# Two chunked recurrences: decay sums, exponentials and weighted operands of a chunk placed in the last steps of the chunk before

## What is computed

```python
def step(state, inp):
    r_t, w_t, k_t, v_t, a_t, b_t = inp
    sa = jnp.einsum('bhvk,bhk->bhv', state, a_t)
    state = (state * w_t[:, :, None, :] + sa[..., None] * b_t[:, :, None, :]
             + v_t[..., None] * k_t[:, :, None, :])
    return state, jnp.einsum('bhvk,bhk->bhv', state, r_t)
...
w = -jax.nn.softplus(-(w0_d + jnp.tanh(dlo) @ w2_d)) - 0.5
decay = jnp.exp(-jnp.exp(w.astype(jnp.float32)))
o = wkv7_scan(rh, heads(decay), kh, vh, -kk, b_vec, reverse)
o = (head_group_norm(o, ln_g, ln_b) + bonus).reshape(B, S, RWKV_WIDTH)
```

## Time and profile before

| | |
|---|---|
| runs of the kernel | 3740.72, 3750.13, 3750.52 us; median 3750.13 us |
| the profiled execution | 3743.04 us, its span 3741.3 us |
| mean granted clock of TensorE | 0.964 |
| PE busy | 3462.3 us, 93% of the span |
| DVE busy | 1727.7 us, 46% |
| ACT busy | 1111.7 us, 30% |
| POOL busy | 329.3 us, 9% |

### The profile page before, as it was taken

How to read it: one execution, slowest core, us unless ns; L and a number is a source line. 1 busy time by engine, 2 the same in 40 slices (tenths; PEclk the granted TensorE clock), 3 DMA queues, 4 the chain that set the end, 5 groups by cost and what they waited for, 6 DMA issues and landing times.

```text
span 3741.3 us, 61040 instructions
## 1 busy us (share of the span) xinstructions
PE 3462.3 (93%) x27176; PEld 2747.7 (73%) x27176; DVE 1727.7 (46%) x2528; ACT 1111.7 (30%) x1789; POOL 329.3 (9%) x342
## 2 busy tenths in 40 slices
PE   8999999889988888898999999989899999999998
PEld 7678677667766775366887788768677778878876
DVE  4443455555555555645334533552454522253235
ACT  4323324333343331022113311333332311132124
POOL 1222231111111111100000000000000000000000
PEclk9999999999998998999999999999999999999999
DMA  3241242211111203321112211222102211121122
GB/s 137 73 131 57 91 168 67 67 46 45 37 56 44 78 25 124 105 94 55 46 51 73 86 50 51 96 92 86 45 30 90 73 45 45 57 90 62 51 68 96
DMA packets 89975, 269.83 MB, mean 72 GB/s; under 512 B 11552, under 2 KB 12080, under 8 KB 89712
## 3 DMA queue, kind: packets, MB, share of 16 engines
q1 hardware_dynamic: 78960, 230.26, 18.6%
q0 software_dynamic: 10752, 35.66, 2.8%
HBM read 219.73 MB, written 46.14 MB: 71 GB/s over the span
## 4 chain that ended last, share of the span: by engine, by line
PE 77%; DVE 10%; issue 7%; ACT 3%; POOL 1%; DMA 1%; SPq 0%; DVEq 0%; POOLq 0%; ACTq 0%
PE ps L355 72%; DVE X L364 3%; PE ps L358 3%; PE ps L354 2%; DVE AR L364 2%; DVE SM L375 1%; POOL AR L364 1%; DVE OTB L364 1%; ACT HH L361 1%; DVE HL L364 1%; ACT W L1966 0%; ACT WS L361 0%; DMA qk_d<-AR 0%; ACT HT L1144 0%; DVE SA L364 0%
## 5 line engine op out<-in xcount | busy, mean ns | idle before, releaser
L355 PE MATMUL ps<-HH,WS 128*128 128x512 f32 (+1 forms) x3232 | 1001.4, 391 | 0.0
L355 PEld LDWEIGHTS ps<-HH,WS 128*128 128x128 f32 (+1 forms) x3232 | 607.8, 188 | 129.9
L355 PE MATMUL ps<-HL,WS 128*128 128x512 f32 x1616 | 639.3, 396 | 10.1 <-DVE HL L364 10.1
L364 DVE TENSOR_TENSOR WS<-W,WS 128x1024 fp32r<-128x1024 f32 (+1 forms) x245 | 300.3, 1226 | 639.5 <-ACT WS L361 639.1
L355 PE MATMUL ps<-WS,SA 128*128 128x512 f32 x2112 | 493.4, 394 | 42.5 <-DVE SA L364 42.5
L361 ACT ACTIVATE WS<-W 128x1024 fp32r<-128x1024 f32 (+1 forms) x245 | 257.6, 1051 | 904.6 <-PE ps L355 892.2
L355 PEld LDWEIGHTS ps<-WS,SA 128*128 128x128 f32 x2112 | 399.3, 190 | 133.8 <-DVE SA L364 31.6
L355 PEld LDWEIGHTS ps<-HL,WS 128*128 128x128 f32 x1616 | 303.8, 188 | 75.1 <-issue 10.5
L355 PE MATMUL ps<-WS,HL 128*128 128x512 f32 x576 | 211.8, 402 | 13.2 <-DVE WS L364 8.7
L355 PE MATMUL ps<-WS,HH 128*128 128x512 f32 x640 | 206.9, 400 | 13.5 <-DVE HL L364 4.8
L355 PE MATMUL ps<-HL,HI 128*128 128x512 f32 (+1 forms) x512 | 209.5, 409 | 3.9 <-POOL WL L364 2.8
(11 more groups left out here) (280 smaller groups left out, 4516.4 us busy)
## 6 DMA issues: line engine op xcount, KB each, us to landing
W<-in_w_fd SPq DMA_DIRECT2D x88, 512.0 KB, 3.3
AR<-rw_d SPq DMA_DIRECT2D x104, 256.0 KB, 4.0
W<-in_w_fg SPq DMA_DIRECT2D x44, 512.0 KB, 3.3
W<-in_w_fu SPq DMA_DIRECT2D x44, 512.0 KB, 3.3
W<-in_w_tok SPq DMA_DIRECT2D x24, 512.0 KB, 3.3
rw_d<-X POOLq DMA_DIRECT2D x40, 256.0 KB, 3.3
X<-in_x SPq DMA_DIRECT2D x16, 512.0 KB, 9.2
W<-in_w_g SPq DMA_DIRECT2D x16, 512.0 KB, 3.7
```

The source lines that it names most:

```text
L355: return pe.e.matmul(o, l, r, start=start, stop=stop)
L364: return e.e.tensor_tensor(o, x, y, op)
```

## The change

A chunk's preparation moves out of its own first step into the last steps (`u` = 1) of the preceding chunk.

- TensorE: the decay sums of chunk i + 1 (`sums`) come behind B, three steps ahead of the chunk's start. The first step of a chunk now has the transposes T0 and T1, the second T2 and T3.
- DVE: the subtraction (`less_own`) is in B's step, the products `At` and `Rt` (`weighed`) in the step of O and U. Removing the mean (`centred`) and summing the squares (`spread`) of chunk i - 1 are behind the copies of T0 and T2 of chunk i.
- ACT: the three exponentials (`exps`) are in B's step, `e2` first; `e1` is written into `c.KT`, which is free by then, since `c.E[1]` is `c.Kt` and still read.
- POOL: `Bt` and `Kt` wait for the state matmuls S of the preceding chunk, which read the same buffers, and no longer for each other; the squares go to `c.D4` and stand behind them.
- SP: the next loads are issued one step later.

The numbers of steps stay, but for one more at the very beginning. Chunk 0 has no preceding chunk: its preparation stands alone in that step.

```diff
                 yield
+                yield
                 if i < 7:
                     sp.wait_ge(*at(f"ve_s{d}", "T", i, 2))
                     sp.wait_ge(*at(f"ae_s{d}", "T", i, 3))
                     sp.wait_ge(*at(f"ge_s{d}", "K", i))
                     load(i + 1)
-                yield
...
-            for i in range(8):
-                v_ = c.vb[i % 2]
+            def sums(i):
                 b = take(pe, PEs, "tc", i)
                 pe.wait_ge(*at(f"dma_ld{d}", i))
                 mm(pe, ps[:, b, :], c.TC, c.sg, True, True).then_inc(*pe.sig(PEs, "tc", i))
-                yield
+
+            sums(0)
+            yield
+            for i in range(8):
+                v_ = c.vb[i % 2]
                 for n, x_ in enumerate((c.At, c.Rt, c.Bt, c.Kt)):
+                    if n == 2:
+                        yield
                     b = take(pe, PEs, "T", i, n)
                     if n < 2:
...
                     for h in range(4):
                         x = mm(pe, ps[src, b, 64 * h:64 * h + 64], c.V2[dst, h, :], c.TT[dst, h, dst], True, True)
                     x.then_inc(*pe.sig(PEs, "B", i, u))
+                    if u and i < 7:
+                        sums(i + 1)
                     yield
                     bo = take(pe, PEs, "O", i, u, n=2)
                     state(pe, c, bo, u, 1)
...
+            def less_own(i):
                 ve.wait_ge(*at(PEs, "tc", i))
                 if i:
-                    ve.wait_ge(*at(VEs, "vr", i - 1))
+                    ve.wait_ge(*at(VEs, "A", i - 1))
                 tt(ve, c.E[2], ps[:, bank(PEs, "tc", i), :], c.sg, ALU.subtract).then_inc(*ve.sig(VEs, "tc", i))
-                yield
+
+            def weighed(i):
                 ve.wait_ge(*at(AEs, "e2", i))
                 ve.wait_ge(*at(f"dma_ld{d}", i))
                 tt(ve, c.At, c.kkn, c.E[2], ALU.mult).then_inc(*ve.sig(VEs, "A", i))
+                ve.wait_ge(*at(AEs, "e0", i))
                 tt(ve, c.Rt, c.r, c.E[0], ALU.mult).then_inc(*ve.sig(VEs, "R", i))
+
...
+            less_own(0)
+            weighed(0)
+            yield
+            for i in range(8):
                 ve.wait_ge(*at(PEs, "T", i, 0))
                 ve.e.tensor_copy(c.ART[:, :, 0, :], hv(bank(PEs, "T", i, 0))).then_inc(
                     *ve.sig(VEs, "T", i, 0, frees=(PEs, "T", i, 0)))
+                if i:
+                    centred(i - 1)
+                yield
                 ve.wait_ge(*at(PEs, "T", i, 2))
                 ve.e.tensor_copy(c.BT, hv(bank(PEs, "T", i, 2))).then_inc(*ve.sig(VEs, "T", i, 2, frees=(PEs, "T", i, 2)))
+                if i:
+                    spread(i - 1)
                 yield
...
                     ve.wait_ge(*at(PEs, "B", i, u))
                     ve.e.tensor_copy(c.TT[src, :, dst], v3(ps[src, bank(PEs, "B", i, u), 0:256], 4)).then_inc(*done("B", i, u))
-                    yield
+                    if u and i < 7:
+                        less_own(i + 1)
+                    yield
+                    if u and i < 7:
+                        weighed(i + 1)
                     yield
...
-                mu, vr = [z[:, d * 64 + t * 8:d * 64 + t * 8 + 8] for z in (MU, VR)]
-                o3 = v3(c.OB, 8)
-                ve.wait_ge(*at(AEs, "O", i, 1))
-                red(ve, mu, o3).then_inc(*ve.sig(VEs, "mu0", i))
-                ve.wait_ge(*at(VEs, "mu0", i))
-                ts(ve, mu, mu, 1.0 / 64, None, ALU.mult, None).then_inc(*ve.sig(VEs, "mu", i))
-                ve.wait_ge(*at(VEs, "mu", i))
-                tt(ve, o3, o3, bl(mu, 64), ALU.subtract).then_inc(*ve.sig(VEs, "om", i))
-                ve.wait_ge(*at(GEs, "o2", i))
-                red(ve, vr, v3(c.E[2], 8)).then_inc(*ve.sig(VEs, "vr", i))
+            centred(7)
+            spread(7)
...
-            for i in range(8):
+            def exps(i):
                 b = bank(PEs, "tc", i)
                 ae.wait_ge(*at(VEs, "tc", i))
+                ae.e.activation(c.E[2], c.E[2], ACT.Exp, scale=-EH).then_inc(*ae.sig(AEs, "e2", i))
                 ae.e.activation(c.E[0], ps[:, b, :], ACT.Exp, scale=-EH).then_inc(*ae.sig(AEs, "e0", i))
-                ae.e.activation(c.E[1], ps[:, b, :], ACT.Exp, scale=EH).then_inc(*ae.sig(AEs, "e1", i, frees=(PEs, "tc", i)))
-                ae.e.activation(c.E[2], c.E[2], ACT.Exp, scale=-EH).then_inc(*ae.sig(AEs, "e2", i))
-                yield
+                if i:
+                    ae.wait_ge(*at(PEs, "M", i - 1, 1, 3))
+                ae.e.activation(c.KT.rearrange("p a b -> p (a b)"), ps[:, b, :], ACT.Exp, scale=EH).then_inc(
+                    *ae.sig(AEs, "e1", i, frees=(PEs, "tc", i)))
+
+            exps(0)
+            yield
+            for i in range(8):
                 ae.wait_ge(*at(PEs, "T", i, 1))
                 cp(ae, c.ART[:, :, 1, :], hv(bank(PEs, "T", i, 1))).then_inc(*ae.sig(AEs, "T", i, 1, frees=(PEs, "T", i, 1)))
+                yield
                 ae.wait_ge(*at(PEs, "T", i, 3))
                 cp(ae, c.KT, hv(bank(PEs, "T", i, 3))).then_inc(*ae.sig(AEs, "T", i, 3, frees=(PEs, "T", i, 3)))
                 yield
...
+                    if i:
+                        ae.wait_ge(*at(VEs, "vr", i - 1))
                     copy(c.D4, two(bank(PEs, "D4", i, u)), "D4", i, u)
...
                     yield
+                    if u and i < 7:
+                        exps(i + 1)
                     yield
                     copy(c.U, hv(bank(PEs, "U", i, u), 256), "U", i, u)
...
+            def squares(i):
+                ge.wait_ge(*at(VEs, "om", i))
+                tt(ge, c.D4.rearrange("p a h (g n) -> p (a h g) n", n=64), v3(c.OB, 8), v3(c.OB, 8),
+                   ALU.mult).then_inc(*ge.sig(GEs, "o2", i))
+
+            yield
             for i in range(8):
-                yield
+                e1 = c.KT.rearrange("p a b -> p (a b)")
                 ge.wait_ge(*at(AEs, "e1", i))
                 ge.wait_ge(*at(f"dma_ld{d}", i))
-                tt(ge, c.Bt, c.bb, c.E[1], ALU.mult).then_inc(*ge.sig(GEs, "B", i))
-                ge.wait_ge(*at(GEs, "B", i))
-                tt(ge, c.Kt, c.k2, c.E[1], ALU.mult).then_inc(*ge.sig(GEs, "K", i))
+                if i:
+                    ge.wait_ge(*at(PEs, "S", i - 1, 1))
+                tt(ge, c.Bt, c.bb, e1, ALU.mult).then_inc(*ge.sig(GEs, "B", i))
+                tt(ge, c.Kt, c.k2, e1, ALU.mult).then_inc(*ge.sig(GEs, "K", i))
+                yield
+                if i:
+                    squares(i - 1)
                 yield
...
-                ge.wait_ge(*at(VEs, "om", i))
-                tt(ge, v3(c.E[2], 8), v3(c.OB, 8), v3(c.OB, 8), ALU.mult).then_inc(*ge.sig(GEs, "o2", i))
+            squares(7)
```

More of the change, by code:

```diff
@@ L1457, in masked @@
                        bc(c.mask2, 2), ALU.mult).then_inc(*ve.sig(VEs, "M", i, u, h, frees=(PEs, "M", i, u, h)))
-            ve.e.memset(c.TT[dst, :, src], 0.0).then_inc(*ve.sig(VEs, "TT0"))
-            for i in range(8):
-                t = tile_of(d, i)
+            def less_own(i):
                 ve.wait_ge(*at(PEs, "tc", i))
                 if i:
-                    ve.wait_ge(*at(VEs, "vr", i - 1))
+                    ve.wait_ge(*at(VEs, "A", i - 1))
                 tt(ve, c.E[2], ps[:, bank(PEs, "tc", i), :], c.sg, ALU.subtract).then_inc(*ve.sig(VEs, "tc", i))
-                yield
+            def weighed(i):
                 ve.wait_ge(*at(AEs, "e2", i))
@@ L1469, in scan_ve, with centred, spread @@
                 tt(ve, c.At, c.kkn, c.E[2], ALU.mult).then_inc(*ve.sig(VEs, "A", i))
+                ve.wait_ge(*at(AEs, "e0", i))
                 tt(ve, c.Rt, c.r, c.E[0], ALU.mult).then_inc(*ve.sig(VEs, "R", i))
+            ve.e.memset(c.TT[dst, :, src], 0.0).then_inc(*ve.sig(VEs, "TT0"))
+            def centred(i):
+                t = tile_of(d, i)
+                mu = MU[:, d * 64 + t * 8:d * 64 + t * 8 + 8]
+                o3 = v3(c.OB, 8)
+                ve.wait_ge(*at(AEs, "O", i, 1))
+                red(ve, mu, o3).then_inc(*ve.sig(VEs, "mu0", i))
+                ve.wait_ge(*at(VEs, "mu0", i))
+                ts(ve, mu, mu, 1.0 / 64, None, ALU.mult, None).then_inc(*ve.sig(VEs, "mu", i))
+                ve.wait_ge(*at(VEs, "mu", i))
+                tt(ve, o3, o3, bl(mu, 64), ALU.subtract).then_inc(*ve.sig(VEs, "om", i))
+            def spread(i):
+                t = tile_of(d, i)
+                ve.wait_ge(*at(GEs, "o2", i))
+                red(ve, VR[:, d * 64 + t * 8:d * 64 + t * 8 + 8], c.D4.rearrange("p a h (g n) -> p (a h g) n", n=64)).then_inc(
+                    *ve.sig(VEs, "vr", i))
+            less_own(0)
+            weighed(0)
+            yield
+            for i in range(8):
                 ve.wait_ge(*at(PEs, "T", i, 0))
```

## The result

The changed kernel takes 3656.13 us (median of 4 runs, 3653.02 to 3656.53), the kernel before beside it 3750.32; the ratio is 0.9752, with a 95% interval of 0.9735 to 0.9770. Forecast were 3672, with a range from 3642 to 3706. The gain is 94 us by the medians and 86.6 us between the two profiled executions (spans of 3741.3 and 3654.7 us). A later set of five executions of the changed kernel has one of 6888 us, which no comparison here uses; the median of its other four is 3658.3 us.

The account below looks back on a forecast made before the run. TensorE, busy 93% of the span, was taken as the bound, standing still at chunk starts for late operands. 63.3 + 2 + 20 - 12 = 73 us off 3743 gives 3670, off the median 3677; forecast 3672, range 3642 to 3706.

Parts of the forecast that it names:

- waits for At and Rt, with the first chunks: TensorE's waits at chunk-start transposes for VectorE's products: 63.3 us go at 14 starts, 2 us more at the first chunks.
- clock: TensorE at chunk starts: without stillness its clock shouldn't fall, so transposes and matmuls behind shorten; 20 us, ends 0 and 28.
- new waits: Moved instructions on DVE, ACT and POOL stand ahead of the other stream's work: 0.85 us per start, 12 us lost.
- Waits that go: At 14 later chunk starts operands are ready when the transposes' turn comes: 63.3 us, 4.5 us each.
- the walk: Step-by-step timing of the chunk start without attention: transposes get about 1.5 us to spare, new waits together 0.9 us.
- The first chunks: First chunk of each direction: two exponentials leave the path to At; 2 us gained of 8.1, ends 0 and 3.
- for them I add 0.1 us each start: Small matmuls behind the chunk-start transposes also leave the slow stretch: 0.1 us per start, 1.5 us in all.
- Rival (a): DVE's queue at the chunk start stands bare 3.0 us at 14 starts, losing 42 us, not 12: 3700; chance 0.17.
- (b): TensorE's short idles suffice to keep its clock low, transposes stay at 0.22 us each: 3690; chance 0.12.
- factor of 1.6: Speedup of chunk-start transposes taken from the rows: 18.5 us won, where a factor of two would give 25 us.
- (c): Slower: every moved instruction on ACT, DVE and POOL lies bare, 8.9 us a start: 3783; chance 0.04.
- (d): More gain: new waits nil and the clock's gain at its end, 63.3 + 3 + 28 = 94 us: 3649; chance 0.09.

Follow-up runs that it names:

- filled kernel: The kernel before with 24 useless identity transposes on TensorE at each of the 14 later chunk starts, ahead of its wait for At: 3728.2 us, ratio 0.9953.

## Why the prediction was right, and where its sizes were off

The forecast was a sum; the two traces give each term of it.

| term | forecast | measured |
|---|---|---|
| waits for At and Rt, with the first chunks | 63.3 + 2 | 71.4 - 4.2 = 67.2 |
| clock | 20 | 805.8 - 775.2 = 30.6 |
| new waits | -12 | 35.4 - 46.0 = -10.6 |
| sum | 73 | 87.2 |

- **Waits that go.** Right at all 14 starts, and the walk fits: it gave the transposes 1.5 us to spare at the thinnest place, and the trace has the products end at 1281.31 and the transposes begin at 1282.78. The first chunks gained more than the 2 us priced, and more than the stated end of 3: 8.1 us became 4.2.
- **The clock** was mis-sized, beyond its stated end of 28, and it is the one term that matters for the miss. The step "for them I add 0.1 us each start" failed. The transposes gave 56.9 - 35.4 = 21.5 us, near the 21.1 by which I priced all 256; I had then taken 14/16 of it, though the first chunks' transposes got faster too. The other 9 us are in all the work behind the transposes that ran in a slow stretch, where I had 1.5. The filled kernel shows the same from outside: 19.2 us from the clock with half of the slow time gone (110 us to about 54).
- **New waits.** The size was right and the place only partly: at the start without attention the walk gave 0.9 us and the trace 0.37, at H2 as said, and none at An. The rest of the 10.6 us is spread over the rounds with attention, which I hadn't walked.
- **Not foreseen:** DVE's scaling of the state beside POOL's products (1.23 us). The walk had the products of POOL collide with nothing.
- **Rival (a)**, DVE's queue giving half of it back, didn't come; the experiment with 2 us more on DVE shows how near it was, for there DVE's queue costs 20 us. **(b)**, the clock low without long waits, fell: 1.00 over 790 us, with some 50 short idles in them. The second failure mode of the Trainium skill (TensorE: Matmul & The Clock Gate, A second HAM failure mode) isn't what happens here. The factor of 1.6 that the prediction set against the factor of two of the Trainium skill (TensorE: Matmul & The Clock Gate, Part 1) was a misreading of mine: it compares means, and the 0.22 us is a mean over slow and fast ones. Start to start the trace has 213 ns at 0.50 and 109 ns at 1.00, and so agrees with a factor of two. Halving all 56.9 us was still too much, for two reasons: 46 of the 254 recorded transposes had been fast before, and the last one of a group, which nothing overlaps, went only from 421 to 273 ns. **(c)** needed 6.1 us a start; the walk's margins held. **(d)**, 3649, is nearer to the time than the forecast: 7 us off and not 16. Its clock term of 28 us was the better one, its new waits of nil were wrong by 10.6 us. That its 94 us are also the difference of the medians is chance, since it counts from the profiled execution, where the gain was 86.6.
- The profiled executions differ by 86.6 us and the medians by 94.2. The 7 us between are the spread of the kernel before, whose profiled run was 7 us under its median. The time lies in the forecast's own band of 3655 to 3685, by 1.1 us.

## What to carry to other kernels

Where engines work through lists in a fixed order, look at the chunk's seam: work that closes one chunk stands in the queue ahead of work that opens the next, and each part of such a chain moved off it counted nearly in full (24 us where 27 and a little clock were expected, 15 us for the order of three exponentials). Price a stillness of TensorE twice, once for the wait and once for the matmuls that follow it at the lower clock; dummy work in the gap shows the second without moving anything, though not all of it (19 of 31 us here). Then ask of each moved instruction what of the other streams stands behind it in its queue: with more work on DVE that, and not the step it prepares, got late first (2.78 us at H1).

## What the runs showed of the hardware

- TensorE's granted clock was low (0.50, 1.2 GHz) behind the waits of each of the 14 later chunk starts, 2.5 to 6.3 us in one or two pieces, and stayed at 2.4 GHz over 790 us with 51 idles of up to 2.1 us (39 us in all). 24 useless transposes in the gap kept it up at 9 of the 14 starts and made the kernel faster. The wait alone doesn't fix it: behind the same 1.73 + 1.11 us at d = 1's first chunk the clock over the next 5 us was 1.00 in the kernel before and 0.66 in the filled one.
- An f32 transpose of 128x128 follows the one before it after 109 ns at the full clock and 213 ns at the half.
- DVE and POOL slow each other when DVE's instruction takes both of its tiles from SBUF. DVE's products of two SBUF operands, 128x512: 1.51 us each beside POOL, 0.64 without; its scaling of 128x128: 1.23 and 0.29; attention's scaling of 128x1024 by a column, both in SBUF: 1.25 and 0.75. An addition with one operand in PSUM (X5, 0.68 to 0.69 us) and the sum over one SBUF tile (0.68) took the same beside POOL and without it. POOL's product: 1.59 to 1.60 us beside two such products of DVE, 1.25 to 1.29 alone.
